# A 31-tap depthwise convolution on TensorE: from pairs of 64x64 tiles, one tap each, to 128x32 tiles that add four taps over shifted copies

## The chip, the cores and the metric

The kernel runs on one core of a Trainium2 chip. The metric is the device time of one execution in microseconds (us), from launch to end; the median of several executions is quoted. The profiled execution is a single one, recorded by the hardware profiler. Its span runs from the first to the last instruction.

## The reference, cut to what matters

Two layers of a small model work on 256 tokens of width 1024 (float32), followed by a second block with attention and 32 experts. Layer 1 begins with a conformer convolution; its depthwise part has 31 taps over time, one weight for each tap and channel:

```python
def causal_dwconv(x, w, b):
    K, C = w.shape
    y = lax.conv_general_dilated(
        x, w[:, None, :], window_strides=(1,), padding=[(K - 1, 0)],
        dimension_numbers=("NWC", "WIO", "NWC"), feature_group_count=C)
    return y + b

def conformer_conv(x, norm, w1, b1, dw_w, dw_b, ln_g, ln_b, w2, b2):
    h = rms_norm(x, norm) @ w1 + b1
    h = jax.nn.glu(h, axis=-1)
    h = causal_dwconv(h, dw_w, dw_b)        # 31 taps, 1024 channels
    h = jax.nn.silu(layer_norm(h, ln_g, ln_b))
    return h @ w2 + b2
```

So out[t, ch] is the sum over k of w[k, ch] times h[t + k - 30, ch], plus a bias. After it come cross attention (its keys and values are projections of `mem`, computed in advance), the feed-forward layer, and the second block.

## The kernel before, in words

**Layout.** Channels lie on the 128 partitions: a tensor of 1024 channels is 8 chunks of [128 channels, 256 tokens]. All weights arrive as one stream of slabs, [128, 1024] float32 or 512 KB each, in the order in which they are used (`PHASES`). SyncE (SP) issues one DMA for each slab in program order (L549), into `raw`, a ring of 12 slabs. A load waits until the slab that held its place has been split or, where slabs are not split, used.

**Split.** A float32 product is made of three passes over rounded parts. ScalarE (ACT) writes the high part `wh` (L636); VectorE (DVE) for even slabs (L1154) and GpSimd (POOL) for odd ones (L1030) write the low part `wl`. Both have 4 places. TensorE (PE) then runs L1864, L1865 and L1866 for column and row slabs, L1949 to L1951 for value slabs. The splits run 3 slabs ahead (`AHEAD`).

**The stretch around the convolution.** PE goes in this order: `pw1` (16 slabs, the two halves of the gated linear unit), `k1` (8 slabs, the next layer's keys), the convolution (`cw`), `v1` (8 value slabs, in two halves of 4), `pw2` (8 slabs). While `pw1` runs, ACT and DVE make the gated result chunk by chunk and DVE writes it to `hpad` (L1519), 30 zero columns ahead of the 256 tokens; semaphore `glu_out` counts the chunks.

**The convolution before.** Chunks 0 and 1 (`OFF_PE = 2`) are made off the array: ACT multiplies `hpad`, shifted by k, by the tap's weights (L821, L824; 62 products) and POOL adds 60 of them (L1122). Chunks 2 to 7 go on PE, in 3 pairs. A tap is a diagonal matrix of weights; each chunk's diagonal is cut into two 64x64 blocks, and the two chunks of a pair give four blocks that occupy the four quarters of the array. That makes 3 pairs x 31 taps x 4 = 372 matmuls at L1983, of 64 rows, 64 columns and 256 tokens, in full float32. Their weights come in 12 slabs (`CW`), used from `raw` without a split. Odd chunks come out with their halves swapped, and the vectors and rows that follow are swapped to match.

**After it.** ACT takes each chunk from PSUM with its bias into `cv` (L834). The mean for the layer norm is a matmul of `cv` with ones (L1995, `ln_mean`), two chunks at a time between convolution slabs, and the last four (chunks 6, 7, 0, 1) after the first value slab. DVE subtracts the mean (L1527), ACT squares (L847), PE sums the squares (L1873), POOL takes the root (L1041), PE spreads it (L1883), and DVE, ACT and DVE make the operands of `pw2` (L1533, L852, L855, L1540). Value slabs fill PE meanwhile.

**Around it.** `slot_of`, `fills_of` and `back_to_same` say in which place of `raw` a slab lies. From `SHORT0` (the start of `win`, rounded up to 12) to `SHORT1` (the start of `moe`, rounded down to 12) the ring has only 6 places, because attention uses the rest. The expert slabs then use a ring of 32 places made of `raw` and of areas that come free.

Of the kernel before, what the change touches and what calls it, by code (L numbers as in the profile page):

```python
# [53 lines left out]
CONV_TAPS = 8  # L54
OFF_PE = 2
CW = 4 * (KC - OFF_PE) // 2
# [15 lines left out]
for _name, _k in PHASES:  # L72
# [7 lines left out]
        ("c_dw_w", 8 * CONV_C), ("c_dw_b", 8), ("c_ln_g", 8), ("c_ln_b", 8), ("c_b_pw2", 8),  # L80
# [220 lines left out]
def program(nc, stream, cols_in, konst_in, masks_in, x_in, mem_in, router_in, out):  # L301
    ctx = ExitStack()
    with ctx:
# [39 lines left out]
        hpad = sb("hpad", "arena", 24, [P, KC, T + CONV_C - 1])  # L343
        tap = sb("tap_products", "arena", 42, [P, 4, T])
# [131 lines left out]
        def taps_until(n):  # L476

            return 4 * max(n - 6, 0) // 3

        def conv_acc(c):  # L480

            return (acc[1], acc[2], acc[3], pw[(USE0["v1"] + 3) % 4])[c % 4]
# [52 lines left out]
        def _(sp):  # L535
# [19 lines left out]
            early, late = S0["cw"] // RAW - 2, -(-(S0["cw"] + CW) // RAW) + 1  # L555
# [68 lines left out]
        def _(act):  # L624
# [186 lines left out]
            def off_taps(lo, hi):  # L811

                for m in range(lo, hi):
                    c, k = m % OFF_PE, m // OFF_PE
                    w, src = col("c_dw_w", c * CONV_C + k), hpad[:, c, k:k + T]
                    if m == 0:
                        act.wait_ge(S("glu_out"), OFF_PE)
                    if m - 4 >= OFF_PE:
                        act.wait_ge(S("tap_added"), m - 4 - OFF_PE + 1)
                    if k == 0:  # L820
                        A.done(act.activation(cv[:, c, :], src, ACT.Identity, scale=w, bias=col("c_dw_b", c)),  # L821
                               S("tap_product"))
                    else:
                        A.done(act.activation(tap[:, m % 4, :], src, ACT.Copy, scale=w), S("tap_product"))  # L824

            for n in range(24):
# [3 lines left out]
                off_taps(taps_until(n), taps_until(n + 1))  # L830
            off_taps(taps_until(24), 37)
            for c in range(OFF_PE, KC):
                wait_slab(act, At(S0["cw"] + 4 * (c // 2 - OFF_PE // 2) + 3))
                A.done(act.activation(cv[:, c, :], conv_acc(c)[:, 0:T], ACT.Identity, bias=col("c_dw_b", c)),  # L834
                       S("conv_out"))
                if c in (OFF_PE + 1, OFF_PE + 3):
                    off_taps(37 + 13 * (c // 2 - OFF_PE // 2), min(50 + 13 * (c // 2 - OFF_PE // 2), 62))
                if c == KC - 5:
                    split(At(S0["v1"]))
                    split(At(S0["v1"] + 1))  # L840
                if c == KC - 3:
                    split(At(S0["v1"] + 2))
                    split(At(S0["v1"] + 3))
# [178 lines left out]
        def _(pool):  # L1022
# [93 lines left out]
            def off_taps(lo, hi):  # L1116

                for m in range(max(lo, OFF_PE), hi):
                    c = m % OFF_PE
                    pool.wait_ge(S("tap_product"), m + 1)  # L1120
                    G.fence(OFF_PE - 1)
                    G.done(pool.tensor_tensor(cv[:, c, :], cv[:, c, :], tap[:, m % 4, :], ALU.add), S("tap_added"))  # L1122

            for n in range(24):
                split(At(S0["pw1"] + n + AHEAD))
                off_taps(taps_until(n), taps_until(n + 1))
            off_taps(taps_until(24), OFF_PE * CONV_C)
# [18 lines left out]
        def _(dve):  # L1146
# [356 lines left out]
            V.fence()  # L1503
            V.done(dve.memset(hpad[:, :, 0:CONV_C - 1], 0.0), S("conv_padding"))
# [1154 lines left out]
```

## Time and profile before

| | us |
|---|---|
| median of 3 executions | 1840.26 |
| lowest, highest | 1838.64, 1845.79 |
| the profiled execution, device time | 1839.95 |
| its span | 1838.2 |

The time of the profiled execution is 1.75 us more than its span, and 0.31 us under the median. Over the span PE is busy 93%, DVE 47%, ACT 36%, POOL 29%. In the page's 40 slices one slice is 46 us; `pw1`, `k1` and the convolution lie in slices 11 to 14, and the experts from slice 29 on, where the DMA line shows 9 and 409 GB/s.

A float32 matmul leaves two LDWEIGHTS and two MATMUL records, each MATMUL record for one half of its passes. "PEld" is the weight load, "PE" the multiplication.

### The profile page before, as it was taken

The numbers are of one execution on the slowest core, as the hardware profiler recorded it, in microseconds if no ns is written. First come the engines' busy times: TensorE is split into PE (matmuls) and PEld (weight loads), VectorE is DVE, ScalarE is ACT, GpSimd is POOL, SyncE is SP. The second block draws the span as 40 slices with busy tenths as digits, with TensorE's granted clock in tenths as the row PEclk, the third lists the DMA queues.
The fourth block names the chain that finished last, engine by engine and source line by source line (L and its number), as shares of the span: only waits on it lengthen the run. The fifth ranks groups of instructions, "written<-read, shape, count | busy, mean of one in ns | idle before, by whom it ended". The sixth has DMA issues, their size and how long they took to land.

```text
span 1838.2 us, 31174 instructions
## 1 busy us (share of the span) xinstructions
PE 1713.1 (93%) x11954; PEld 1383.8 (75%) x11954; DVE 861.1 (47%) x1409; ACT 657.1 (36%) x1127; POOL 536.1 (29%) x329
## 2 busy tenths in 40 slices
PE   7998989999999998999998999987889999989886
PEld 7887979999998797999998998877844444333333
DVE  2787447888772353588785335765411011000002
ACT  2383444444455544434433334654311111111101
POOL 0443424555467431355552443221100000000000
PEclk9999999999899989999997999998889999999997
DMA  7464523555554442355551554333779999999992
GB/s 268 153 206 152 179 92 125 185 180 177 166 167 132 161 161 82 126 186 180 174 187 40 171 185 151 101 104 125 280 307 409 409 409 409 409 410 409 409 409 91
DMA packets 108973, 398.79 MB, mean 217 GB/s; under 512 B 12097, under 2 KB 12353, under 8 KB 108481
## 3 DMA queue, kind: packets, MB, share of 16 engines
q1 hardware_dynamic: 107856, 393.26, 58.9%
q10 hardware_dynamic: 1008, 4.08, 0.6%
q8 instruction: 68, 1.11, 0.3%
q14 instruction: 41, 0.33, 0.1%
HBM read 396.25 MB, written 1.05 MB: 216 GB/s over the span
## 4 chain that ended last, share of the span: by engine, by line
PE 38%; issue 31%; DVE 23%; ACT 6%; POOL 1%; DVEq 1%; DMA 0%; ACTq 0%; SPq 0%; POOLq 0%
DVE wl L1154 6%; DVE cf L1455 5%; PE pw L1864 5%; PE pw L1865 5%; PE pw L1866 5%; ACT wh L636 4%; PE pw L2114 4%; DVE hid L1471 3%; PE acc L1864 3%; PE acc L1865 3%; PE acc L1866 3%; DVE cf L1458 3%; PE acc L1873 3%; PE acc L1983 2%; DVE gpad L1449 1%
## 5 line engine op out<-in xcount | busy, mean ns | idle before, releaser
L1030 POOL TENSOR_TENSOR wl<-raw,wh 128x1024 fp32r<-128x1024 f32 x165 | 402.7, 2441 | 516.0 <-ACT wh L636 515.3
L636 ACT ACTIVATE wh<-raw 128x1024 fp32r<-128x1024 f32 x330 | 342.2, 1053 | 257.6 <-PE pw L1866 151.3
L1864 PE MATMUL pw<-ah,wh 128*128 128x256 f32 x1416 | 410.2, 290 | 4.0 <-DVE gt L1604 4.0
L1865 PE MATMUL pw<-ah,wl 128*128 128x256 f32 x1416 | 406.0, 287 | 0.0
L1866 PE MATMUL pw<-al,wh 128*128 128x256 f32 x1416 | 405.7, 287 | 0.0
L1154 DVE TENSOR_TENSOR wl<-raw,wh 128x1024 fp32r<-128x1024 f32 x165 | 214.6, 1301 | 235.9 <-ACT wh L636 235.8
L1864 PEld LDWEIGHTS pw<-ah,wh 128*128 128x128 f32 x1416 | 277.6, 196 | 8.2 <-issue 6.8
L1865 PEld LDWEIGHTS pw<-ah,wl 128*128 128x128 f32 x1416 | 277.4, 196 | 0.0
L1866 PEld LDWEIGHTS pw<-al,wh 128*128 128x128 f32 x1416 | 277.2, 196 | 0.0
L1864 PE MATMUL acc<-yh,wh 128*128 128x256 f32 x832 | 245.5, 295 | 23.7 <-POOL yl L1099 5.4
L1865 PE MATMUL acc<-yh,wl 128*128 128x256 f32 x832 | 242.2, 291 | 0.0
L1866 PE MATMUL acc<-yl,wh 128*128 128x256 f32 x832 | 241.7, 291 | 0.0
L1041 POOL TENSOR_TENSOR small<-small 128x2 f32<-128x2 f32 x12 | 8.3, 694 | 630.8 <-DVE small L1164 630.8
L1864 PEld LDWEIGHTS acc<-yh,wh 128*128 128x128 f32 x832 | 166.6, 200 | 27.1 <-issue 9.3
L1866 PEld LDWEIGHTS acc<-yl,wh 128*128 128x128 f32 x832 | 166.7, 200 | 0.0
L1865 PEld LDWEIGHTS acc<-yh,wl 128*128 128x128 f32 x832 | 166.3, 200 | 0.1
L1816 DVE COPY slot_gate<-pw 64x1 f32<-64x1 f32 x32 | 5.0, 156 | 253.2 <-ACT slots_to_tokens L977 252.7
L2348 PE MATMUL pw<-raw,gathered 128*64 128x512 f32 x408 | 96.8, 602 | 6.5 <-DMA raw<-in_stream 5.7
L1455 DVE TENSOR_SCALAR cf<-gpad,cols 128x256 f32<-128x256 f32 x48 | 92.3, 1922 | 7.5 <-DVE gpad L1449 6.9
L1099 POOL TENSOR_TENSOR yl<-hid,yh 128x256 fp32r<-128x256 f32 x48 | 51.7, 1077 | 111.9 <-ACT yh L778 111.9
L2114 PE MATMUL pw<-x_gained,raw 128*128 128x256 f32 x320 | 74.8, 397 | 9.5 <-DMA raw<-in_stream 9.5
L774 ACT ACTIVATE cf<-cf 128x256 f32<-128x256 f32 x48 | 20.2, 420 | 172.3 <-DVE cf L1458 172.3
(296 smaller groups left out, 2561.9 us busy)
## 6 DMA issues: line engine op xcount, KB each, us to landing
raw<-in_stream SPq DMA_DIRECT2D x506, 512.0 KB, 3.7
ring_w<-in_stream SPq DMA_DIRECT2D x96, 512.0 KB, 12.8
ring_y<-in_stream SPq DMA_DIRECT2D x72, 512.0 KB, 13.9
ring_m<-in_stream SPq DMA_DIRECT2D x48, 512.0 KB, 12.9
ring_h<-in_stream SPq DMA_DIRECT2D x24, 512.0 KB, 13.7
mem_t<-in_mem ACTq DMA_DIRECT2D x2, 1024.0 KB, 9.4
x_res<-in_x SPq DMA_DIRECT2D x2, 512.0 KB, 6.3
out<-x_res SPq DMA_DIRECT2D x1, 1024.0 KB, 3.9
```

The source lines that it names most:

```text
L636: A.done(act.activation(wh[:, s.base % SPLIT, :], raw[:, slot_of(s.base), :], ACT.Copy), w_hi)
L1030: G.done(pool.tensor_tensor(wl[:, s.base % SPLIT, :], raw[:, slot_of(s.base), :], wh[:, s.base % SPLIT, :].bitcast(F32), ALU.subtract), w_ ...
L1154: V.done(dve.tensor_tensor(wl[:, s.base % SPLIT, :], raw[:, slot_of(s.base), :], wh[:, s.base % SPLIT, :].bitcast(F32), ALU.subtract), w_lo_v)
L1455: V.done(dve.tensor_scalar(cf[:, j % 2, :], gpad[:, j % 2, 2:T + 2], w, col(f"f_dw_b{l}", j, 4, i), ALU.mult, ALU.add))
L1458: V.done(dve.scalar_tensor_tensor(cf[:, j % 2, :], gpad[:, j % 2, 2 - k:T + 2 - k], w, cf[:, j % 2, :], ALU.mult, ALU.add), S("ffn_conv") ...
L1471: V.done(dve.tensor_tensor(hid[:, j % 2, :], cf[:, j % 2, :], uf[:, j % 2, :], ALU.mult), S("ffn_hidden"))
L1864: pe.matmul(dst, wh[:, s.base % SPLIT, w], hi, start=start, stop=False, **kw)
L1865: pe.matmul(dst, wl[:, s.base % SPLIT, w], hi, start=False, stop=False, **kw)
L1866: return pe.matmul(dst, wh[:, s.base % SPLIT, w], lo, start=False, stop=stop, **kw)
L1873: last = pe.matmul(acc[bank][:, q:q + 1], src[:, c, q * P:q * P + P], ones[:, 0:1], start=(c == 0 and q == 0), stop=(c == KC - 1), skip_gr ...
L2114: last = pe.matmul(pw[u % 4][:, 0:T], raw[:, slot_of(n), k * P:k * P + P], ax[:, k, :], start=(k == 0), stop=(k == KC - 1))
L2348: ins = pe.matmul(pw[bank + h][rows, :], stationary(e), ring[(s.base + e - S0["moe"]) % RING][:, 512 * h:512 * h + 512], start=first, stop ...
```

## The change

The convolution is rewritten for all 8 chunks:

- **Shifted copies.** 32 channels of a chunk are put four times on the 128 partitions, the copy number `turn` starting `turn` tokens later. One matmul with 128 rows and 32 columns (four 32x32 diagonals, one under the other) then adds the four taps 4j to 4j+3 of 32 channels. A chunk takes 4 blocks of 32 channels x 8 steps = 32 matmuls (the 32nd tap has weight zero), 256 in all. The four blocks go to the four 32-column strips of the array.
- **The copies are DMAs from `hpad`,** 16 for chunks 0 to 4 into `shifted0` (over `yh` and `yl`) and 16 for chunks 5 to 7 into `shifted1` (over `ah` and `al`). SP issues them between its slab loads, the first 16 behind the load of the first `cw` slab and a wait for `glu_out` 5, the others behind five more loads and waits for `glu_out` 8 and for the last `pw1` slab to be done.
- **`CW` falls from 12 slabs to 8,** one for each chunk. Every slab number from `v1` on is 4 lower.
- **ACT's 62 products and POOL's 60 adds go,** with the 248 columns of tap weights in `cols` and the swapped halves.
- **`ln_mean`** runs one chunk at a time, two chunks behind the convolution; only chunks 6 and 7 are left for after the first value slab. The convolution uses banks `acc[1]` to `acc[3]` and no `pw` bank, and the wait for drained `pw` banks ahead of it goes.
- **ACT splits `v1` 0 to 3** ahead of the first chunk's `conv_out` instead of between them.

The diff, cut (`_swapped` and its uses are dropped as well):

```diff
@@ the constants
-CONV_TAPS = 8
-OFF_PE = 2
-CW = 4 * (KC - OFF_PE) // 2
+TURNS, STEPS = 4, 8
+CW = KC
+EARLY_C = 5
...
@@ the tiles
-        hpad = sb("hpad", "arena", 24, [P, KC, T + CONV_C - 1])
-        tap = sb("tap_products", "arena", 42, [P, 4, T])
+        hpad = sb("hpad", "arena", 24, [P, KC, T + CONV_C])
+        shifted0 = sb("shifted0", "yh", 0, [P, EARLY_C, TURNS, T + CONV_C - TURNS + 1])
+        shifted1 = sb("shifted1", "ah", 0, [P, KC - EARLY_C, TURNS, T + CONV_C - TURNS + 1])
...
@@ SP
+            def shift_out(lo, hi, dst, landed):
+                n = T + CONV_C - TURNS + 1
+                sp.wait_ge(S("glu_out"), hi)
+                for turn in range(TURNS):
+                    for b in range(P // 32):
+                        sp.dma_start(dst[32 * turn:32 * turn + 32, :, b, :],
+                                     hpad[32 * b:32 * b + 32, lo:hi, turn:turn + n]).then_inc(landed, 16)
...
             for s in range((early + 3) * RAW, late * RAW):
                 load(At(s))
+                if s == S0["k1"] + RAW - 4:
+                    sp.wait_ge(S("conv_padding"), 1)
+                    shift_out(0, EARLY_C, shifted0, S("shifted0_in"))
+                if s == S0["k1"] + RAW + 1:
+                    wait_slab(sp, At(S0["pw1"] + 15))
+                    shift_out(EARLY_C, KC, shifted1, S("shifted1_in"))
...
@@ ACT
-                off_taps(taps_until(n), taps_until(n + 1))
-            off_taps(taps_until(24), 37)
-            for c in range(OFF_PE, KC):
-                wait_slab(act, At(S0["cw"] + 4 * (c // 2 - OFF_PE // 2) + 3))
+            for n in range(4):
+                split(At(S0["v1"] + n))
+            for c in range(KC):
+                wait_slab(act, At(S0["cw"] + c))
                 A.done(act.activation(cv[:, c, :], conv_acc(c)[:, 0:T], ACT.Identity, bias=col("c_dw_b", c)),
                        S("conv_out"))
...
@@ PE
-                drain(USE0["v1"])
                 pe.wait_ge(acc_out, KC * ACCS["pw2"])
                 pe.wait_ge(rstd_b_ready, NORMS["c"] + 1)
+                for c in range(KC):
+                    s = At(S0["cw"] + c)
+                    if c in (0, EARLY_C):
+                        pe.wait_ge(S("shifted1_in" if c else "shifted0_in"), 16 * TURNS * P // 32)
+                    if c >= 3:
+                        pe.wait_ge(S("conv_out"), c - 2)
                     wait_raw(pe, s)
+                    for j in range(STEPS):
+                        for b in range(P // 32):
+                            w = (j * 4 + b) * 32
+                            ins = pe.matmul(conv_acc(c)[32 * b:32 * b + 32, 0:T], raw[:, slot_of(s.base), w:w + 32],
+                                            shifted(c)[:, b, TURNS * j:TURNS * j + T], start=(j == 0),
+                                            stop=(j == STEPS - 1), skip_group_check=True)
                     ins.then_inc(slab_done, 1)
+                    if c >= 2:
+                        ln_mean(c - 2)
```

On PE, the rows of the kernel before at the end of the first pair's slabs, around the first means and at the start of the second pair's are these:

```order
L1983 MATMUL pw<-hpad,raw 64x256 x2
L1983 MATMUL acc<-hpad,raw 64x256 x32
L1995 MATMUL acc<-cv,ones 128x256 x2
L1983 MATMUL acc<-hpad,raw 64x256 x94
L1983 MATMUL pw<-hpad,raw 64x256 x2
```

and the whole convolution of the changed kernel, from the last `k1` matmul to the first value matmul, less these two, is this (`shifted_76` and `shifted_77` are `shifted0` and `shifted1`):

```order
L1968 MATMUL acc<-shifted_76,raw 32x256 x96
L1950 MATMUL acc<-cv,ones 128x256
L1968 MATMUL acc<-shifted_76,raw 32x256 x32
L1950 MATMUL acc<-cv,ones 128x256
L1968 MATMUL acc<-shifted_76,raw 32x256 x32
L1950 MATMUL acc<-cv,ones 128x256
L1968 MATMUL acc<-shifted_77,raw 32x256 x32
L1950 MATMUL acc<-cv,ones 128x256
L1968 MATMUL acc<-shifted_77,raw 32x256 x32
L1950 MATMUL acc<-cv,ones 128x256
L1968 MATMUL acc<-shifted_77,raw 32x256 x32
L1950 MATMUL acc<-cv,ones 128x256
```

372 small matmuls with two pairs of means between them became 256 with six single means between or behind them.

On SP, behind the loop that loads the earlier slabs, the kernel before issues only loads:

```order
L549 ISA
L549 DMA raw<-in_stream 128x1024
L556 REGISTER_ALU
L556 COMPARE_AND_BRANCH
L549 DMA raw<-in_stream 128x1024 x24
L561 UNCONDITIONAL_BRANCH
```

and the changed kernel has the 32 copies among them:

```order
L566 REGISTER_ALU
L566 COMPARE_AND_BRANCH
L550 DMA raw<-in_stream 128x1024 x9
L562 DMA shifted_76<-hpad 32x5x284 x16
L550 DMA raw<-in_stream 128x1024 x5
L562 DMA shifted_77<-hpad 32x3x284 x16
L550 DMA raw<-in_stream 128x1024 x22
L577 UNCONDITIONAL_BRANCH
```

The loads of the last seven `cw` slabs and of all `v1` slabs now stand behind one or both groups of copies; the loop ahead of them has one trip less and the straight stretch 12 loads more.

## Rows read from the trace of the kernel before

**Rows 1.** The page, part 2: PE's busy tenths and GB/s in 40 slices.
```profile
PE   7998989999999998999998999987889999989886
...
GB/s 268 153 206 152 179 92 125 185 180 177 166 167 132 161 161 82 126 186 180 174 187 40 171 185 151 101 104 125 280 307 409 409 409 409 409 410 409 409 409 91
```

**Rows 2.** Windows: length, busy of each engine, granted TensorE clock, DMA share, GB/s.
```profile
540.00:560.00 20.00, 20.00 (x169) 20.00 (x169) 16.05 (x17) 12.48 (x19) 18.24 (x13) 1.00 0.59 197
...
590.00:605.00 15.00, 15.00 (x268) 10.30 (x264) 1.62 (x1) 9.13 (x19) 10.34 (x14) 1.00 0.46 154
...
617.00:640.00 23.00, 23.00 (x126) 19.25 (x119) 8.16 (x20) 10.63 (x19) 4.55 (x3) 0.93 0.47 168
```

**Rows 3.** PE's own waits from 500 to 660 us: total, times, longest.
```profile
PE acc L1864 <- DVE wl L1154: 0.5, 1, 0.5
PE acc L1983 <- DVE k_t L1211: 0.5, 1, 0.5
PE acc L1883 <- DVE diag L1171: 0.2, 1, 0.2
```

**Rows 4.** The convolution's instructions: ns min/median/max, first and last start, form.
```profile
L1983 PE MATMUL acc<-hpad,raw x496: 373/375/427, 574.9 to 617.4; 64*64 64x256 f32 x166
L1983 PE MATMUL pw<-hpad,raw x248: 373/375/427, 575.0 to 617.4; 64*64 64x256 f32 x124
```

**Rows 5.** Timeline of PE (start, us, instructions): entry, two means between slabs, exit.
```profile
574.14 0.28 PE L1866 MATMUL pw<-ml,wh 128*128 128x256 f32 x1
574.94 0.43 PE L1983 MATMUL acc<-hpad,raw 64*64 64x256 f32 x2 [0.52 <-DVE k_t L1211]
...
588.38 3.64 PE L1983 MATMUL acc<-hpad,raw 64*64 64x256 f32 x64
591.95 1.13 PE L1995 MATMUL acc<-cv,ones 128*128 128x256 f32 x4
...
617.40 0.39 PE L1983 MATMUL pw<-hpad,raw 64*64 64x256 f32 x2
617.71 0.50 PE L1949 MATMUL pw<-wh,mh 128*128 128x512 f32 x1
...
620.57 1.89 PE L1995 MATMUL acc<-cv,ones 128*128 128x256 f32 x8
622.11 0.58 PE L1949 MATMUL pw<-wh,mh 128*128 128x512 f32 x1
```

**Rows 6.** The critical chain: convolution slabs behind the first detour (start, us, what, count).
```profile
593.08 10.30 PE acc L1983 x186
```

**Rows 7.** Timeline of PE: two bursts of expert matmuls, 128 rows by 64 columns.
```profile
1406.30 1.94 PE L2348 MATMUL pw<-ring_y,gathered 128*64 128x512 f32 x8
1408.06 1.89 PE L2348 MATMUL pw<-ring_w,gathered 128*64 128x512 f32 x8
```

**Rows 8.** Weight loads of 64 and of 128 columns: ns min/median/max.
```profile
L2348 PEld LDWEIGHTS pw<-ring_y,gathered x192: 132/137/137, 1363.5 to 1754.8; 128*64 128x64 f32 x192
L1995 PEld LDWEIGHTS acc<-cv,ones x16: 186/190/190, 591.9 to 621.9; 128*128 128x128 f32 x16
```

**Rows 9.** DVE's writes of chunks 4 and 7 to hpad (timeline).
```profile
538.21 0.85 DVE L1519 SCALAR_TENSOR_TENSOR hpad<-t,cols,t 128x256 f32<-128x256 f32 x1
555.21 0.85 DVE L1519 SCALAR_TENSOR_TENSOR hpad<-t,cols,t 128x256 f32<-128x256 f32 x1
```

**Rows 10.** SP's slab loads: ns to issue; their time from issue to landing.
```profile
L549 SPq DMA_DIRECT2D raw<-in_stream x362: 327/333/1053, 1.6 to 1277.4; - x181
DMA to landing us min/median/max: 3.0/3.3/19.2
```

**Rows 11.** Timeline of SP where the experts begin; then windows of the experts.
```profile
1328.24 0.80 SPq L596 DMA_DIRECT2D ring_h<-in_stream  x2
1346.52 4.24 SPq L596 DMA_DIRECT2D raw<-in_stream  x6
...
1380.00:1400.00 20.00, 20.00 (x101) 7.96 (x98) 2.82 (x6) 2.28 (x4) 0.00 (x0) 1.00 1.03 409
```

More of the change, by code:

```diff
@@ L474, in gather_bank, with shifted @@
             return j if j < 4 else 3 - j % 2
-        def taps_until(n):
-            return 4 * max(n - 6, 0) // 3
+        def shifted(c):
+            return shifted0[:, c, :, :] if c < EARLY_C else shifted1[:, c - EARLY_C, :, :]
         def conv_acc(c):
-            return (acc[1], acc[2], acc[3], pw[(USE0["v1"] + 3) % 4])[c % 4]
+            return acc[1 + c % 3]
         def expert_at(n):
@@ L809, in glu_tanh @@
                 A.done(act.activation(tb, tb, ACT.Tanh, bias=hbc[:, c:c + 1], scale=0.5), S("glu_tanh"))
[L811 to L824, printed above, removed]
             for n in range(24):
@@ L1961, in values, with ln_mean, conv @@
                         hook(kk)
-            def conv(hook):
-                drain(USE0["v1"])
+            def ln_mean(c):
+                pe.wait_ge(S("conv_out"), c + 1)
+                last = pe.matmul(acc[0][:, 0:T], ones[:], cv[:, c, :], start=(c == 0), stop=(c == KC - 1))
+                if c == KC - 1:
+                    last.then_inc(S("ln_mean"), 1)
+            def conv():
                 pe.wait_ge(acc_out, KC * ACCS["pw2"])
                 pe.wait_ge(rstd_b_ready, NORMS["c"] + 1)
-                for n in range(CW):
-                    s, pair = At(S0["cw"] + n), OFF_PE // 2 + n // 4
-                    if n % 4 == 0:
-                        pe.wait_ge(S("conv_padding"), 1)
-                        pe.wait_ge(S("glu_out"), 2 * pair + 2)
-                        if n >= 8:
-                            pe.wait_ge(S("conv_out"), 2 * (n // 4) - 2)
-                    wait_raw(pe, s)
-                    for j in range(min(CONV_TAPS, CONV_C - CONV_TAPS * (n % 4))):
-                        k = CONV_TAPS * (n % 4) + j
-                        for c in (2 * pair, 2 * pair + 1):
-                            for half in range(2):
-                                src = slice(64 * half, 64 * half + 64)
-                                to = 64 * (half ^ c % 2)
-                                w = 2 * j * 64 + 64 * (c % 2)
-                                ins = pe.matmul(conv_acc(c)[to:to + 64, 0:T], raw[src, slot_of(s.base), w:w + 64],
-                                                hpad[src, c, k:k + T], start=(k == 0), stop=(k == CONV_C - 1),
-                                                skip_group_check=True)
-                    ins.then_inc(slab_done, 1)
-                    hook(n)
@@ L2009, in ln_hook @@
                     ln_mean(KC - 1)
-                    for c in range(OFF_PE):
-                        ln_mean(c)
                 if kk == 2:
@@ L2536, in _glu_slabs @@
     return out
-def _swapped(v):
-    v = v.copy()
-    for c in range(OFF_PE + 1, KC, 2):
-        v[c * P:c * P + P] = np.concatenate([v[c * P + 64:c * P + P], v[c * P:c * P + 64]])
-    return v
-def _conv_slabs(w):
-    out = np.zeros((CW, P, 2 * CONV_TAPS, 64), np.float32)
-    p = np.arange(P)
-    for n in range(CW):
-        for j in range(min(CONV_TAPS, CONV_C - CONV_TAPS * (n % 4))):
-            for e in range(2):
-                c = OFF_PE + 2 * (n // 4) + e
-                out[n, p, 2 * j + e, p % 64] = w[CONV_TAPS * (n % 4) + j, c * P:c * P + P]
+def _conv_slabs(w):
+    out = np.zeros((CW, TURNS, 32, STEPS, P // 32, 32), np.float32)
+    i = np.arange(32)
+    for c in range(CW):
+        for k in range(CONV_C):
+            for b in range(P // 32):
+                out[c, k % TURNS, i, k // TURNS, b, i] = w[k, c * P + 32 * b + i]
     return out.reshape(CW, P, SLAB)
```

43 lines of the change are left out of this document (8 added, 35 removed).

## The prediction

> **What bounds the kernel now.** I read the slices first, then the windows around the convolution, then PE's waits there, then the timeline. The slices split the program in two: up to slice 28 PE is busy nearly all the time and DMA moves 40 to 280 GB/s; from slice 30 on DMA stands at 409 GB/s [rows 1]. Between them lies the joint that decides whether time saved early reaches the end. SP has filled the ring of 32 expert slabs at 1328.2 us and issues the next slab only at 1346.5, when PE has used the first one [rows 11]. The rest, 384 - 32 = 352 slabs at 512 KB / 409 GB/s = 1.28 us, is 451 us of transfers from there. So the end hangs on when PE reaches the experts, and PE on all that it did before: a microsecond taken from PE at 600 us is one at the end, if PE doesn't wait instead.
>
> In the stretch of the change PE has no slack. It is busy 20.0 of 20 us and 15.0 of 15 us, at a granted clock of 1.00, and even in the layer norm behind the convolution 23.0 of 23 us [rows 2]; from 500 to 660 us it waits 1.2 us in all [rows 3]. So the count of array microseconds is the sum. ACT and POOL are not the bound: they are busy 9.1 and 10.3 of 15 us beside PE [rows 2], so the 62 products and 60 adds that go are worth nothing by themselves; PE's work covers them. Were PE faster than POOL they would count, and they are gone just then.
>
> **What PE does before.** 372 matmuls are 496 + 248 = 744 MATMUL records of 375 ns [rows 4]. They overlap: 186 starts take 10.30 us, less the last one's 0.375, by 185 gaps: 0.0537 us [rows 6]. Four quarters of the array thus work side by side, each for 0.215 us on an instruction. I take 0.054. 744 x 0.054 = 40.2 us. A detour to the means: the 64 records from 588.38 end at 592.02, so the last starts at 591.65 and the next one would at 591.70; it starts at 593.01 [rows 5]. That is 1.31 us, of which the four records (two means) are 4 x 0.213 = 0.85 (eight of them at the end took 622.11 - 620.57, about as much each [rows 5]) and 0.46 the change of shape, out and back. Two detours, 2.6 us. Entry: the last `k1` matmul starts at 574.14, its successor could at 574.26, the first of the convolution starts at 574.94, behind a wait of 0.52 for DVE's copy of the last `k1` bank. Exit: value work starts at 617.71. From 574.26 to 617.71 are 43.45 us = 0.68 + 40.2 + 2.6 and a rest of nothing.
>
> **What PE does after, part by part.**
> - Matmuls: 256, 512 records. No row has a 128x32 shape. The nearest below: four tiles side by side, as now, 0.054 us each, 27.65 us. The nearest above: the expert matmuls, 128 rows by 64 columns, two strips. Eight records of 512 columns start 1408.06 - 1406.30 = 1.76 us before the next eight [rows 7]: 0.22 each, where one strip alone would need 2 x 0.215 = 0.43. So column strips with all 128 rows do work side by side, two of them; four are not shown. I take 0.054, since both shapes that split the array run at their full share. For two side by side see below.
> - Entry: the wait for `pw` banks goes; 0.2 for the change of shape (of 0.46 for both ways).
> - Means: five come between chunks, one each: 0.43 + 0.46 = 0.89, 4.45 in all. The sixth follows the last chunk: 0.26 + 0.43 = 0.69. That is more than before (5.1 against 2.6), since each trip now carries one mean. If a single trip cost only its 0.43, 2.3 less; if a full 1.31, 2.1 more.
> - Sum: 0.2 + 27.65 + 4.45 + 0.69 = 33.0 against 43.45: 10.45 less. After the first value slab two means stand in place of four: half of 1.54, 0.77 less. In all **11.2 us less**.
> - The waits inside: from chunk 3 on PE wants the chunk three back taken by ACT, and a mean wants the one two back. A chunk is 32 x 2 x 0.054 = 3.5 us and ACT needs under 0.5 for it, with nothing else to do once four splits of 1.06 us are over; the last of them waits for the last `k1` slab, so all are done some 1.5 us into the convolution. Free.
> - Behind the convolution everything keeps its order: centre, squares, sums, root, spread. The chain starts as much earlier as PE does, and the value slabs still cover it; nothing is late that wasn't.
>
> **The copies.** SP waits for chunk 4, written at 539.06 [rows 9], then issues 16 DMAs at 0.33 us or more [rows 10], 5.3 us and up; chunk 7 is there at 556.06 and the other 16 follow. No row has a copy from SBUF to SBUF, nor runs of 284 x 4 = 1136 bytes. Each DMA has 32 x 5 or 32 x 3 runs, 4096 in all, 4.65 MB, 160 + 96 = 256 runs on each of 16 DMA engines. By bytes, at the experts' 409 GB/s, a run is 1136 / 25.6 GB/s = 0.044 us; if a run costs as much as a slab's row of 4096 bytes, 0.16. The first group then takes 7 or 26 us and has landed, with about 3 us of latency [rows 10], at 549 or 568; PE wants it at 574.5. The second lands at 565 or, behind the rest, about 590; PE wants chunk 5 at 594 (574.5 and five chunks of 3.46 and three detours of 0.89). So PE waits for no copy at either end. Cost 0; I hold it to be nearer the cheap end, as DMA is busy only 0.59 at 197 GB/s there [rows 2]. SP's other loads stand behind the copies: `cw` slabs 1 to 7 and the `v1` slabs. The former are wanted 3.5 us apart from 578 on. The latter are a rival.
>
> **The rest.** `CW` shortens the ring's part before `win` by 12 slabs, so 6 places serve from the start of `win`: a load has 6 slabs of 2.9 us to land in and takes 3.3 in the median [rows 10]. The expert ring begins with 2 `raw` places and gets 10 later, in place of 6 and 6; all 16 first slabs must still be there before the last `wout` slab, as now. 127 KB less of `cols` at the start is 0.3 us at most. I count all three as 0.
>
> **Sum.** 1839.95 - 11.2 = 1828.75 for an execution like the profiled one, and as the median stands 0.3 higher, **1829.1 us**, 0.6% less.
>
> **The rivals.**
> - *Weight loads come to light* (chance 0.07). Four strips share all 128 rows, and their weights are changed every 0.215 us. A load of 64 columns takes 0.136, one of 128 takes 0.190 [rows 8], so 32 columns are about 0.03 us of pure loading; if none of it hides, 512 x 0.03 = 15.4 more: 1844.5, no change to speak of. Against it: the expert strips share their rows too, with 0.22 us for each record of 0.215, so their loads do hide [rows 7]. The Trainium skill (TensorE: Matmul & The Clock Gate, Part 3: Packing small matmuls) says that a weight load overlaps matmuls in flight only when its row group differs, which here is never so. By that rule it would be this rival; the trace speaks against it.
> - *Four strips are fed as two* (0.11). The 64x64 tiles read 64 partitions for each of four streams; these read 128 for each of four, and the trace shows 128 for two only. If two is the limit, a record takes 0.108 us: 512 x 0.108 = 55.3, 27.65 more than my sum: **1856.8, slower**. It decides from 0.076 us a record on, where the gain is used up. For it only that no row shows four; against it that strips of 64 columns lose nothing.
> - *A late `v1` slab stops ACT* (0.13). ACT now splits `v1` 0 to 3 ahead of the first `conv_out`. PE goes to the first mean after three chunks, at 574.5 + 10.4 = 584.9, and for that ACT must have chunk 0, so `v1` 3 must land by 583.3. From 539.1 the DMA engines have 44 us for 256 runs and 11 slabs (`cw` 1 to 7, `v1` 0 to 3; 14.1 us): it decides from (44 - 14.1) / 256 = 0.117 us a run. At 0.16 the slab is 11 us late, and so is all behind it: 1840, the same as now. The Trainium skill (DMA: Bandwidth & Descriptors, Why small descriptors are slow) says that small descriptors are penalised with HBM only, not from SBUF to SBUF; no row here shows it.
> - *The gain is given back* by something I counted as 0 (0.04): spread over the range.
>
> **How the numbers follow.** My case has 0.65. Its own range is 1826.5 to 1834: the trips at 0.43 or 1.31 (-2.3, +2.1), a record at 0.058 (+2.1), `cols` (-0.3). 8 in 10 need about 0.15 more above: with the late slab at 1840 and the exposed loads at 1844.5 the range is **1826.5 to 1844.5**; the slower case lies outside. 0.5% (9.2 us) is about what a measurement of this kernel can tell from no change: that is 1831.1 and 1849.5. Of my case 0.53 lies below 1831.1 and 0.12 above; late slab, exposed loads and a part of the rest are same: 0.33. Slower: 0.14.
>
> **What would show it.** Right: 512 MATMUL records of 128x32 that start 0.054 us apart, value work some 33 us after the last `k1` matmul, PE waits under 1 us there, the first group landed before 570, and the experts' first reload 11 us earlier than 1346.5. Wrong: records 0.108 apart, or gaps of 0.1 us with PE waiting for nothing (fed as two, or loads); PE waiting for `shifted` tiles or for `cv`, with ACT's splits behind a `raw` DMA (late slab); a granted clock under 1.00 there.

## The result, and the profile after

| us | before | after |
|---|---|---|
| median | 1839.85 (4 executions) | 1822.13 (4 executions) |
| lowest, highest | 1838.64, 1845.79 | 1820.92, 1823.83 |
| the profiled execution, and its span | 1839.95, 1838.2 | 1822.83, 1821.0 |

The ratio of the times is 0.9909, with a 95% interval of 0.9885 to 0.9933. The changed kernel is 17.7 us faster; 11 were forecast, and the time lies below the range.

**The convolution did what was forecast.** The answer to [rows 4]: the instructions on the `shifted` tiles of the changed kernel (ns min/median/max, first and last start, form), then the latency of the copies.

```profile
L1968 PEld LDWEIGHTS acc<-shifted,raw x512: 106/110/110, 574.2 to 605.3; 128*32 128x32 f32 x171
L1968 PE MATMUL acc<-shifted,raw x512: 379/379/403, 574.2 to 605.5; 128*32 128x256 f32 x171
L562 SPq DMA_DIRECT2D shifted<-hpad x32: 592/606/1022, 538.3 to 565.7; - x32
...
DMA to landing us min/median/max: 3.1/5.9/8.0
```

The answer to [rows 5], PE's timeline of the changed kernel: start, us, instructions.

```profile
574.00 0.28 PE L1850 MATMUL pw<-ml,wh 128*128 128x256 f32 x1
574.20 10.57 PE L1968 MATMUL acc<-shifted,raw 128*32 128x256 f32 x192
584.70 0.70 PE L1950 MATMUL acc<-cv,ones 128*128 128x256 f32 x2
585.33 3.66 PE L1968 MATMUL acc<-shifted,raw 128*32 128x256 f32 x64
588.92 0.70 PE L1950 MATMUL acc<-cv,ones 128*128 128x256 f32 x2
589.55 3.66 PE L1968 MATMUL acc<-shifted,raw 128*32 128x256 f32 x64
...
605.80 0.70 PE L1950 MATMUL acc<-cv,ones 128*128 128x256 f32 x2
606.15 0.58 PE L1933 MATMUL pw<-wh,mh 128*128 128x512 f32 x1
```

192 records start in 10.57 - 0.38 us, 0.0534 apart. The last `k1` matmul starts at 574.00, so its successor could at 574.12; value work starts at 606.15. That is 32.0 us where [rows 5] had 43.45.

**The gain reaches the experts with 1.6 us less, and then grows.** Each layer norm ends in a root on POOL (L1041 before, L1034 after). Its start is a mark that every kernel has (us from the start of the profiled execution):

| root of | before | after | gained so far | in this stretch |
|---|---|---|---|---|
| the convolution's input | 503.33 | 503.02 | 0.31 | 0.31 |
| the layer norm behind the convolution | 631.65 | 619.77 | 11.88 | 11.57 |
| second cross attention | 679.27 | 668.06 | 11.21 | -0.67 |
| the mixing step | 991.67 | 980.43 | 11.24 | 0.03 |
| the experts | 1318.35 | 1308.11 | 10.24 | -1.00 |
| the output | 1827.55 | 1810.43 | 17.12 | **6.88** |

The last two rows, before and then after. In brackets stands how long POOL sat idle ahead of the root: for the last one that is the length of the whole expert stretch, and one row tells it for any kernel.

```profile
1318.35 0.69 POOL L1041 TENSOR_TENSOR small<-small 128x2 f32<-128x2 f32 x1 [11.62 <-DVE small L1164]
1827.55 0.69 POOL L1041 TENSOR_TENSOR small<-small 128x2 f32<-128x2 f32 x1 [508.51 <-DVE small L1164]
```

```profile
1308.11 0.69 POOL L1034 TENSOR_TENSOR small<-small 128x2 f32<-128x2 f32 x1 [11.63 <-DVE small L1147]
1810.43 0.69 POOL L1034 TENSOR_TENSOR small<-small 128x2 f32<-128x2 f32 x1 [501.63 <-DVE small L1147]
```

No line of the experts' work was changed, and yet they take 6.9 us less. SP's timeline shows where. Before, at each return to the last two places of the ring (32 slabs further each time):

```profile
1540.32 2.66 SPq L596 DMA_DIRECT2D ring_h<-in_stream  x2
1582.29 2.05 SPq L596 DMA_DIRECT2D ring_h<-in_stream  x2
1623.95 2.05 SPq L596 DMA_DIRECT2D ring_h<-in_stream  x2
1666.76 2.67 SPq L596 DMA_DIRECT2D ring_h<-in_stream  x2
...
1791.88 2.20 SPq L596 DMA_DIRECT2D ring_h<-in_stream  x2
```

and after:

```profile
1528.67 1.99 SPq L612 DMA_DIRECT2D ring_h<-in_stream  x2
1569.57 2.05 SPq L612 DMA_DIRECT2D ring_h<-in_stream  x2
1610.53 2.05 SPq L612 DMA_DIRECT2D ring_h<-in_stream  x2
1651.55 1.99 SPq L612 DMA_DIRECT2D ring_h<-in_stream  x2
...
1774.13 2.20 SPq L612 DMA_DIRECT2D ring_h<-in_stream  x2
```

Six rounds of the ring took 1791.88 - 1540.32 = 251.56 us before, 41.9 each, and 245.46 after, 40.9 each, which is 32 x 1.28. The rate of all DMA is the same in both, 409 to 410 GB/s. The difference is in the instruction queue. The view of DMA over these six rounds, before:

```profile
DMA packets 28263, 102.99 MB, mean 409 GB/s; under 512 B 3137, under 2 KB 3137, under 8 KB 28253
## 3 DMA queue, kind: packets, MB, share of 16 engines
q1 hardware_dynamic: 28253, 102.89, 102.6%
q14 instruction: 8, 0.07, 0.1%
```

and after:

```profile
DMA packets 27597, 100.53 MB, mean 410 GB/s; under 512 B 3063, under 2 KB 3063, under 8 KB 27594
## 3 DMA queue, kind: packets, MB, share of 16 engines
q1 hardware_dynamic: 27594, 100.49, 102.7%
...
q14 instruction: 1, 0.01, 0.0%
```

### The profile page after: what moved, and what is told of

It is laid out like the page before. It is cut to its first block, busy times and chain, and to the rows that moved or that the text cites. A ratio compares the mean times of both kernels' runs of the same rounds, so it can differ in the third digit from the quotient of the medians.

```text
span 1821.0 us, 30499 instructions
## 1 busy us (share of the span) xinstructions
PE 1703.2 (94%) x11722; PEld 1373.0 (75%) x11722; DVE 859.4 (47%) x1410; ACT 628.7 (35%) x1067; POOL 487.7 (27%) x269
## 4 chain that ended last, share of the span: by engine, by line
PE 37%; issue 31%; DVE 23%; ACT 7%; POOL 1%; DVEq 1%; DMA 0%; ACTq 0%; SPq 0%; POOLq 0%
DVE wl L1137 6%; DVE cf L1438 5%; PE pw L1848 5%; PE pw L1849 5%; PE pw L1850 5%; ACT wh L652 4%; PE pw L2082 4%; DVE hid L1454 3%; PE acc L1848 3%; PE acc L1850 3%; PE acc L1849 3%; DVE cf L1441 3%; PE acc L1857 2%; PE acc L1968 2%; DVE gpad L1432 1%
## 5 line engine op out<-in xcount | busy, mean ns | idle before, releaser
L1034 POOL TENSOR_TENSOR small<-small 128x2 f32<-128x2 f32 x12 | 8.3, 691 | 622.7 <-DVE small L1147 622.7
```

## Experiments

**1. Move SyncE's loop in the kernel before.** Waits that are long fulfilled serve as padding; two of them fold to one instruction:

```diff
             for s in range((early + 3) * RAW, late * RAW):
                 load(At(s))
+                if s == S0["k1"] + RAW:
+                    for _ in range(110):
+                        sp.wait_ge(S("conv_padding"), 1)
```

> The kernel before with 110 waits on a semaphore that has long been raised, written on SyncE's queue behind one load of the ring (they fold to 55 instructions), and nothing else changed. It moves SyncE's expert loop from its instructions 273 to 498 to 328 to 553, where the changed kernel has it. Background: of the 17.7 us that were gained only 10.3 were there when the experts began; the other 7 came between 1590 and 1810 us, where the stream of slabs runs at 409 GB/s in both kernels, but in the kernel before one DMA engine falls behind the other 15 and packets of the instruction queue q14 (8192 bytes) come 4 or 5 times in each trip of the expert loop, in the changed one hardly. Theory A (code placement: some engine's expert loop is fetched again in every trip, and each fetch holds one DMA engine up by about 0.7 us): if it is SyncE's code, the packets in the stretch go and the time falls by 5 to 8 us, 1832 to 1835; if it is another engine's, 1839 to 1841. Rival B (the order of the places in the expert ring) and rival C (4 slabs fewer in the stream): no change, within 1 us of before.

Measured: 1831.99 us (5 executions) against 1840.32 of the kernel before beside it; ratio 0.9959 (0.9940 to 0.9978). 8.3 us by doing nothing 110 times, with an interval of 4 to 11 us. The surer reading is the expert stretch, in brackets, 7.6 us shorter than the 508.51 before:

```profile
1819.58 0.69 POOL L1045 TENSOR_TENSOR small<-small 128x2 f32<-128x2 f32 x1 [500.94 <-DVE small L1168]
```

The same six rounds of the ring take 245.51 us, and the DMA view of them has no q14 packet at all:

```profile
q1 hardware_dynamic: 27612, 100.54, 102.7%
q8 instruction: 1, 0.02, 0.0%
```

The lag of the last part stays at 0.1 us from 1443 to 1795. So it is SyncE's code, unless the padding itself did it by the pause that it makes; experiment 3 tests that. Rivals B and C, the order of places and the number of slabs, didn't change here, and fall.

**2. Move ScalarE's loop in the kernel before.**

```diff
             off_taps(taps_until(24), 37)
+            for _ in range(136):
+                act.wait_ge(S("conv_padding"), 1)
```

> The kernel before with 136 such waits on ScalarE ahead of its first read of a convolution bank (68 instructions), which moves ScalarE's expert loop from instructions 1152 to 1207 to 1220 to 1275, the same place within 128 instructions as in the changed kernel. Theory A: if the packets of q14 are ScalarE's, they go from the experts and the time falls by 5 to 8 us; if they are SyncE's, nothing changes. Rivals B and C: no change. The waits themselves stand in ScalarE's slack and cost at most 1 us.

Measured: 1837.99 us (10 executions), ratio 0.9987 (0.9965 to 1.0009), no difference that can be told. The expert stretch is as before, with seven q14 packets from 1590 to 1780:

```profile
1826.87 0.69 POOL L1044 TENSOR_TENSOR small<-small 128x2 f32<-128x2 f32 x1 [508.60 <-DVE small L1167]
```

**3. A control for the padding.** As experiment 1, with 256 waits.

> A control for the padding: the kernel before with 256 waits on SyncE in place of 110, at the same spot. They fold to 128 instructions, so its expert loop stands at 401 to 626, 128 further than before and in the same place within 128. Theory (the place of SyncE's loop within 128 instructions decides whether its code is fetched again in each trip): the five fetches a trip are there and the time is that of before, 1838 to 1842. Rival (the padding itself, by the pause of some 8 us that it puts between SyncE's loads, is what gained 8 us with 110 waits): the gain is there again, 1830 to 1834, or greater. If 128 is not the period, the fetches go.

Measured: 1839.73 us (10 executions), ratio 0.9990 (0.9976 to 1.0004). The fetches are back at the same points of the loop, 8 packets in six rounds of 251.61 us:

```profile
1831.20 0.69 POOL L1045 TENSOR_TENSOR small<-small 128x2 f32<-128x2 f32 x1 [507.25 <-DVE small L1168]
```

So it isn't the padding but the place. 128 instructions further on the loop is fetched as it was; whether a shorter step would do the same, this one pair doesn't tell.

**4. The changed kernel with the loops where they were before.** The same padding on SyncE (73 instructions) and ScalarE (60).

> The changed kernel with waits as padding on SyncE (73 instructions) and on ScalarE (60), so that both expert loops stand within their 128 instructions just as in the kernel before. Theory A, whether SyncE's or ScalarE's code is the cause: the packets of q14 come back among the experts and 5 to 8 us are lost, 1827 to 1830. Rivals B and C, and code of another engine: 1821 to 1824.

Measured: 1828.55 us (4 executions), ratio 0.9943 (0.9924 to 0.9962); 6.4 us of the changed kernel's gain are gone, and q14 packets come at five times in the second trip again. The two intervals just overlap, but the expert stretch is 507.81 us against 501.63. This is the change without its luck, 0.5 us under the forecast, and it includes 1.5 us that the padding itself cost (see experiment 6).

```profile
1817.28 0.69 POOL L1040 TENSOR_TENSOR small<-small 128x2 f32<-128x2 f32 x1 [507.81 <-DVE small L1153]
```

**5. The place between.** The changed kernel with 74 waits on SyncE, 37 instructions.

> The changed kernel with 37 instructions of folded waits on SyncE ahead of the v1 slabs: its expert loop of 225 instructions stands at 365 to 590, between the place of the changed kernel (328 to 553, no repeated fetches, about 1822) and that of the padded one (401 to 626, five in each trip, 1828.6). Theory (placement within blocks of 128 instructions decides): either none or all of the five fetches a trip and 6 us, nothing between; a place whose end falls in the same block as at 553 should have none: 1821 to 1825. If each instruction of shift costs, it is 3 us more than the changed kernel, 1825.

Measured: 1819.76 us (4 executions), ratio 0.9889 (0.9858 to 0.9920), expert stretch 500.89, three q14 packets in the loop's first trip, none in the second and one in the third. Nothing between, then: with its first instruction at 319 (experiment 6), 328 or 365 the loop of 225 instructions is hardly fetched again, at 273 and 401 five times a trip. Where in between it turns wasn't tried.

**6. The old numbering and the old order of the ring.**

```diff
-CW = KC
+CW = 12
...
+def conv_slab(c):
+    return S0["cw"] + (2 * c if c < 4 else c + 4)
```

(and the waits and weights to match).

> The changed kernel with its convolution weights spread over 12 slabs (chunks 0 to 3 take two half-empty slabs each), so that every slab number, the short ring, the order of the expert ring's places and the place of every slab in memory are as in the kernel before. SyncE's expert loop moves by 9 instructions. Theory A: the 7 us stay gained, 1821 to 1824. Rivals B and C: they come back, 1828 to 1831.

Measured: 1819.38 us (4 executions), ratio 0.9897 (0.9880 to 0.9914). The 7 us stay gained with the stream and the ring of the kernel before (expert stretch 500.05); that settles rivals B and C a second time. It showed something else too. PE's waits from 570 to 640 us in this kernel:

```profile
PE acc L1954 <- ACT cv L839: 3.0, 1, 3.0
```

and ACT there:

```profile
582.64 1.06 ACT L656 ACTIVATE wh<-raw 128x1024 fp32r<-128x1024 f32 x1 [18.61 <-DMA raw<-in_stream]
583.89 1.06 ACT L656 ACTIVATE wh<-raw 128x1024 fp32r<-128x1024 f32 x1 [0.19 <-DMA raw<-in_stream]
...
587.37 1.19 ACT L839 ACTIVATE cv<-acc,cols 128x256 f32<-128x256 f32 x3
```

This is the rival "a late `v1` slab stops ACT", at work. ACT waits 18.6 us for `v1` slabs, because SP issues them behind 32 copies and, here, four more `cw` slabs; so it takes the first bank at 587.4, and PE, which wanted it at 584.9, waits. (Still the median is 2.8 us under the changed kernel's: between kernels that were not measured beside each other, whole times don't tell 3 us apart.) In the changed kernel itself the same row reads:

```profile
577.31 1.06 ACT L652 ACTIVATE wh<-raw 128x1024 fp32r<-128x1024 f32 x1 [13.39 <-DMA raw<-in_stream]
...
582.03 0.82 ACT L835 ACTIVATE cv<-acc,cols 128x256 f32<-128x256 f32 x2
584.84 0.47 ACT L835 ACTIVATE cv<-acc,cols 128x256 f32<-128x256 f32 x1 [1.99 <-PE acc L1968]
```

It has chunk 0 out by 582.5, 2.2 us before PE's first mean at 584.70. The padding of experiment 4, which stands ahead of these loads, used that up as well: PE waited 1.5 us there.

**7. Without the copies.** SP issues waits in their place, and the matmuls read `hpad`.

```diff
-                for turn in range(TURNS):
-                    for b in range(P // 32):
-                        sp.dma_start(dst[32 * turn:32 * turn + 32, :, b, :],
-                                     hpad[32 * b:32 * b + 32, lo:hi, turn:turn + n]).then_inc(landed, 16)
+                for _ in range(32):
+                    sp.wait_ge(S("conv_padding"), 1)
...
-                                            shifted(c)[:, b, TURNS * j:TURNS * j + T], start=(j == 0),
+                                            hpad[:, c, TURNS * j:TURNS * j + T], start=(j == 0),
```

> The changed kernel without its 32 copies: SyncE issues folded waits in their place (16 instructions for each group of 16 DMAs, so that its expert loop stays where it is), and TensorE's 256 matmuls read hpad itself in the same shape. The shifted copies are left out, so the convolution sums other channels and times than it should; the work on the array is the same in count and shape. Theory (copies are free: they land 7 us or more ahead of TensorE, but they hold SyncE for 22 us, so the first four v1 slabs land late and ScalarE's splits end at 582.1, 2.6 us ahead of the first mean): the convolution's own 32.0 us from the last k1 matmul to the value work do not change by more than 0.3, ScalarE's splits end some 15 to 20 us earlier, and the end is the same within 2 us. Rival (the copies slow the slabs and matmuls around them): the stretch from 500 to 606 us becomes shorter by 1 us or more, and the end with it.

Measured: 1823.19 us (4 executions), ratio 0.9902 (0.9874 to 0.9929), 1.1 above the changed kernel. From its first convolution matmul (578.14) to value work (610.10) are 31.96 us; in the changed kernel 606.15 - 574.20 = 31.95. The copies cost nothing in the stretch, and the 1.1 us at the end lie inside the intervals. ACT's last split ends 1.2 us into the convolution in place of 7.9: 6.7 us earlier, and not the 15 to 20 that I had expected, because then it waits for PE to give back its places.

**8. Two strips by turns, and 9. one strip after the other.**

```diff
-                    for j in range(STEPS):
-                        for b in range(P // 32):
+                    for pair in range(2):
+                        for j, b in [(j, 2 * pair + e) for j in range(STEPS) for e in range(2)]:
```

> The changed kernel with the 32 matmuls of a chunk in another order: all 16 of strips 0 and 1 by turns, then all 16 of strips 2 and 3, in place of four strips by turns. Count, shapes, weights and result are the same. Theory (strips work side by side, each for 0.215 us on a record, and a weight load hides behind the other strips' matmuls): two at a time give 0.107 us a record in place of 0.0534, so 512 x 0.054 = 27.4 us more, about 1849.5. Rival (what sets 0.0534 is the issue of instructions, not the strips): less than 5 us more. If weight loads of 32 columns were exposed once only one other strip is busy, it would be more than 0.12 a record, 1855 and above.

> The changed kernel with the 32 matmuls of a chunk ordered strip by strip: all 8 of strip 0, then of strip 1, 2 and 3. Two strips by turns gave pairs of records 0.216 us apart, 0.108 a record, with some overlap where one pair of strips handed over to the next: 6.27 us a chunk in place of 3.66. Theory (a strip takes 0.216 us for a record, whatever the others do): 8 matmuls of two records are 3.45 us on a strip, 13.8 us a chunk, less the overlap of three handovers (0.3 us each): about 12.9 in place of 3.4, 75 us more in eight chunks, 1897. Rival (the load of weights is exposed when no other strip works beside it, some 0.03 to 0.1 us for each record): 15 to 50 us above that, 1912 and more.

A chunk of 64 records, with two strips by turns:

```profile
598.94 6.27 PE L1968 MATMUL acc<-shifted,raw 128*32 128x256 f32 x64
```

with one after the other:

```profile
614.29 11.50 PE L1968 MATMUL acc<-shifted,raw 128*32 128x256 f32 x64
```

and 3.66 with four. From the first convolution matmul to value work: 51.2 us (581.60 to 632.83), 93.0 (581.27 to 674.30), and 31.95. The single records show why. Inside a strip each starts 0.216 us after the one ahead of it, in all three kernels. Four strips by turns start four records 7 ns apart and then wait out the 0.216; two start two. Where one strip hands over to the next, the first records of the new one slip in beside the last of the old, nearly 4 of them at each handover (0.8 us saved, where I had reckoned 0.3); so 64 records in one row take 11.5 us and not 12.9. The whole times are 1834.72 us (11 executions; ratio 0.9967, 0.9953 to 0.9981) and 1881.44 (2 executions; 1.0222, 1.0170 to 1.0273). I had 1849.5 and 1897. The stretch grew by 19.3 us and 61.1, where 27.4 and 75 were expected. The end of the first grew by only 12.6; its profiled execution was its slowest, 1847.92, and had lost 7.3 us before the convolution began, so where the others made up 6 us can't be read from it. From the root of the convolution's input to the last root it took 17.8 us more than the changed kernel, so there the growth of the stretch did reach the end.

A load of 32 columns (110 ns) shows in none of them: 0.216 us a record in one strip, with new weights for each matmul, is four times the 0.054 of [rows 6], where four tiles share the time.

**10. The means in one row.** The changed kernel makes six trips to `ln_mean`.

```diff
-                    if c >= 2:
-                        ln_mean(c - 2)
+                for c in range(KC - 2):
+                    ln_mean(c)
```

> The changed kernel with the means of chunks 0 to 5 in one row behind the last chunk in place of one between two chunks. A trip from one chunk to the next over one mean measured 0.80 us, of which the two records of the mean are 0.43 and the change of shape 0.37. Theory: five of the six changes of shape go, 5 x 0.37 = 1.9 us less at the value work (32.0 becomes 30.1), and at the end, since TensorE is the path up to the experts: 1820.2; dips of the granted clock between 980 and 1310 us move single kernels by up to 3 us either way, so the sharper reading is the stretch. Rival (the end of the chain, squares and root behind the means, gets the gain or ScalarE is late with a bank): the stretch shortens, the layer norm's root does not come earlier.

```profile
575.40 27.83 PE L1968 MATMUL acc<-shifted,raw 128*32 128x256 f32 x512
603.17 2.86 PE L1950 MATMUL acc<-cv,ones 128*128 128x256 f32 x12
605.67 0.58 PE L1933 MATMUL pw<-wh,mh 128*128 128x512 f32 x1
```

Measured: **1818.28 us** (4 executions), ratio 0.9874 (0.9846 to 0.9901). That is faster than the kernel before. Against the changed kernel the intervals overlap, and the kernel of experiment 5, which has the changed kernel's means, measured 1819.76 beside it; so the whole time doesn't show this gain. The stretch does: from the first convolution matmul to value work are 30.27 us, 1.68 less. The root of the layer norm comes 114.73 us behind that of the convolution's input, in place of 116.75, and the next one 161.90 in place of 165.04. So the rest gained another 1.5 us rather than eating this one. Most of that lies behind the root, where the granted clock differs. These are the windows around the stretch at its lower level (1.2 GHz), before, after and here (columns as in [rows 2]):

```profile
631.00:636.00 5.00, 5.00 (x19) 4.03 (x19) 0.64 (x3) 0.00 (x0) 0.70 (x1) 0.66 0.20 79
618.00:627.00 9.00, 9.00 (x33) 7.57 (x33) 2.00 (x7) 0.54 (x2) 0.69 (x1) 0.62 0.14 54
619.00:625.00 6.00, 6.00 (x23) 4.86 (x22) 1.91 (x6) 0.54 (x1) 0.56 (x1) 0.72 0.01 4
```

A mean of 0.62 over 9 us is 6.8 us at half speed; 0.66 over 5 us and 0.72 over 6 are 3.4. In all three PE was busy without a gap ahead of it, and had just passed the matmuls that sum the squares. From this root to the next the three kernels with 6.8 us there took 48.3 us, those with 3.4 took 47.1 to 47.6, and that of experiment 6, with no such stretch there, 45.0. That the clock makes this difference is argued from these numbers; no experiment set it alone.

## Why the prediction was wrong

Step by step, as it stands above:

- **The bound: right up to the experts.** PE carried the gain to them, and the first reload came at 1336.27 in place of 1346.52 [rows 11], 10.25 us earlier where 11 were forecast. "A microsecond taken from PE at 600 us is one at the end" held up to there, within 1.6 us.
- **Matmuls: right.** 512 records 0.0534 us apart (0.054). Four strips with all 128 rows work side by side. The rival "four strips are fed as two" is out, and experiment 8 shows what it would have cost at least: two by turns are 19.3 us more, with some overlap at the handovers.
- **Weight loads: hidden.** The rival is out. The Trainium skill (TensorE: Matmul & The Clock Gate, Part 3: Packing small matmuls) lets a load overlap only when its row group differs. These 512 loads all have the same one, all rows, and experiment 9 even changes weights inside one strip each time without a gap. The measurement decides against that rule for this case.
- **Means: 0.80 us a trip, 0.89 forecast.** A chunk starts 4.22 us after the one ahead of it (589.55 - 585.33), less 64 x 0.0534 = 3.42. The first trip took 0.88. Over five trips that is 0.4 us less.
- **The sum of the stretch: 32.0 us, 33.0 forecast.** 0.4 from the trips, 0.3 from the records (512 x 0.0534 = 27.3), 0.1 from entry (0.08 in place of 0.2) and 0.2 from the last mean (602.21 + 64 x 0.0534 = 605.63, and 606.15 less that is 0.52, in place of 0.69). Right in kind.
- **Copies: free, as forecast, by a wrong rate.** SP needs 11.68 us for 16 of them, not 5.3: 0.6 us of issuing each and 0.73 from one to the next, where a slab has 0.33 [rows 10]. The last one was issued at 565.7, and none took more than 8 us to land; PE came to chunk 5 at 593.77. The packet records of the 4096 runs last 0.094 us in the mean (0.048 to 0.168). That is twice the 0.044 by bytes that I held for likelier, and not far under the deciding 0.117.
- **The splits: wrong.** "The last of them waits for the last `k1` slab, so all are done some 1.5 us into the convolution": it was 7.9 us, on account of `v1` slabs that landed late. The rival that I gave 0.13 missed the changed kernel by 2.2 us, and cost 1.5 us in experiment 4 and 3.0 in experiment 6. The forecast priced transfers and not SP's issuing, which is 22 us of the queue ahead of these slabs. That PE never waited was so partly by luck.
- **Given back: 1.6 us** between 620 and 1308 (0.67 from the layer norm's root to the next, 1.00 behind the mixing step, rounded). I had 0. In the first the granted clock stood at its lower level for 6.8 us, and for 3.4 us in the kernel before (experiment 10). The second lies in a stretch where the granted clock changes between its two levels several times, and its length varies among kernels that have the same instructions there: 326.7 us before, 327.7 after, 322.1 in experiment 1, 324.1 with 37 instructions of padding.
- **The failed step: "The rest, 352 slabs at 512 KB / 409 GB/s = 1.28 us, is 451 us of transfers from there",** taken as the same on both sides. It is true of the changed kernel, 40.9 us for 32 slabs. The kernel before took 41.9, though its rate was 409 GB/s too. It lost 6.1 us in six rounds that had 8 fetches of SyncE's code. The changed kernel doesn't lose them, and that is the gain that the sum had at nothing. I read the mean rate of 16 engines as the rate at which slabs arrive, and did not hold it against the spacing of SP's issues, which the same trace shows. Had I done so, the extra microsecond of each round would have been in view ahead of time; not, though, that this change would take it away.

With SyncE's loop back in its old place the change measured 1828.55; the forecast was 1829.1. In the other order, from the kernel before with the loop moved (1831.99) to the changed one (1822.13), it is 9.9. So of 17.7 us some 10 to 12, by either order, are the convolution's and 6 to 8 come from where a loop happened to stand. The traces agree: 10.24 us at the root of the experts and 6.88 behind it. That loop's place was luck. Without it the time would have come within some 2 us of the forecast, though the prices of the copies' runs and of the splits would still have been wrong.

## What to carry to other kernels

Hold the time between two landmarks of a transfer-bound stretch against slabs x bytes / rate: if it is longer at full rate, look whether the last part of each transfer lands ever later than the others, and at the small instruction queues. An edit anywhere ahead of a loop, on the queue that issues the transfers, can move the loop by some instructions and so change the time of a stretch that it doesn't touch; before a difference is put down to the edit, move the loop alone by padding, in both kernels. For matmuls of 128 rows by 32 columns, order them so that consecutive ones go to different strips: the same 256 matmuls took 32, 51 or 93 us by their order alone. When DMAs are put on a queue, count the issuing, 0.6 to 0.7 us each here, against whatever stands behind them.

## What the runs showed of the hardware

- **Whether a loop on SyncE of 225 instructions is fetched again in every trip goes by its place.** Starts at 273 and 401: five times of fetching in the second and in the third trip of some 126 us, expert stretch by POOL's row 507.2 to 508.6 us. Starts at 319, 328 and 365: none in the second trip and at most one in the third, trips of 122.9 us, 500.0 to 502.4. Positions are counted in the built program of SyncE, without what the runtime puts ahead of it.
- **Each of these fetches costs 0.76 us in a saturated stretch** (251.56 less the 245.51 us of experiment 1, for 8 packets), though a packet of 8192 bytes is 0.32 us of one engine at 409 / 16 = 25.6 GB/s. Why it is more stays open. The steps of the lag say the same, 0.3 to 0.9 us at each packet; that the fetches cause it rests on experiments 1, 3 and 4.
- The Trainium skill (Runtime: NRT & Kernel Launch, Instruction fetch mechanics) says that a taken branch whose target lies outside the two pages held forces a fetch of the target. That fits a loop fetched again in each trip. It gives 16 KiB and 256 instructions for a page; the q14 packets here are of 8192 bytes, half of it. Why there are five fetches is not explained: the trace has some 320 SyncE instructions in a trip (the program counts 225), and three or four pieces of 128 would hold either.
- **A strip of 128 rows by 32 columns takes 0.216 us for a float32 record of 256 columns, with one, two or four strips at work,** and its next weights are loaded in that time.
- **DMAs from SBUF to SBUF with runs of 1136 bytes took 0.094 us a run,** 12 GB/s on an engine, where the slabs' rows of 4096 bytes ran at 25.6.
- **Executions differ by some microseconds before the change even begins.** The root of the convolution's input came at 502.0 to 510.3 us in the 12 profiled executions, of kernels with nearly the same instructions up to there, and the kernel before ranged from 1836.61 to 1847.32 over 14 executions. What sets it wasn't looked into.
